# First projection of a diffusion layer: conditioning weights for shift and scale read in eight blocks, norm sums as columns

## The chip, the cores and the metric

The kernel runs as one program on one core of a Trainium2 chip. The core has a matrix engine (TensorE, "PE"), a vector engine (VectorE, "DVE"), a scalar engine with function tables (ScalarE, "ACT"), a general engine (GpSimd, "POOL") and a queue engine (SyncE, "SP"), which here only issues transfers. All work on tiles of up to 128 partitions in on-chip memory (sb); matrix products land in eight banks of 128 x 512 fp32. The metric is the device time of one execution in microseconds (us), the median of several runs.

## The reference

One layer of a diffusion backbone: 256 latent tokens and 256 context tokens of width 1024, all in fp32. What matters here is how the layer's input is made, ahead of three mixing branches and a mixture of experts:

```python
def rmsnorm(x, g):
    y = xf * lax.rsqrt(jnp.mean(xf * xf, axis=-1, keepdims=True) + RMS_EPS)
    return (y * g)
def modulate(h, shift, scale):
    return h * (1 + scale) + shift
# m = silu(c) @ w_ada + b_ada, six vectors of 1024: shift and scale of the mixer come first
# h = modulate(rmsnorm(x, g_mix), shift, scale), for latents with c, for context with c_ctx
zl = split_in(h_lat @ w_in)      # w_in is 1024 x 7936
zc = split_in(h_ctx @ w_in)
```

The first two groups of w_in's columns that the kernel uses are the two forget gates of a gated scan ("ff" and "fb"), 512 columns each.

## The kernel before, in words

The tokens are held transposed: hT has 8 feature blocks (k = 0 to 7, 128 features on the partitions) by 512 tokens. Every weight group is 1024 x 512 (2 MB) and is read into one of three rotating slots of sb. SP issues these reads in the order of the list FRONT; before a slot is taken again it waits until TensorE has used it (`w_used`). TensorE makes a group's output in "fills": a fill is one bank of 128 x 512, the sum over the 8 feature blocks. Each fp32 matmul stands in the trace as two records, a transpose as one. There is no scheduler: each engine's program is written out in order, and semaphores hold the engines together.

The start is this. ACT takes silu of the conditioning vectors (line 511) and squares hT block by block (line 515). TensorE sums the squares over the features with a matrix of ones (line 884), 8 matmuls of 128 x 512, so that each partition holds all 512 sums as a row. ACT takes the root (line 518), DVE the reciprocal of 128 x 512 (line 1142) and multiplies each block by it (line 1166). The conditioning product for shift (w_ada groups ada0, ada1) and scale (ada2, ada3), 512 columns each, is 8 matmuls per group with a stationary operand of only 32 columns (line 695), four such groups of columns of the array running side by side; ACT copies the result (line 535), four transposes bring it onto partitions (line 845), DVE sums the four parts (line 1160), adds the bias and makes the factor A_mix (lines 1171 to 1175), and applies factor and shift to hT in two halves of 256 tokens (line 1179). Half of the features (k = 0 to 3) is served by ada0 and ada2, the other half by ada1 and ada3. So TensorE's order is: ada0, ada2, their transposes, the first half of k for the first three tiles of ff, then ada1, ada3, their transposes, then the second half of k, ff's fourth tile, fb and onwards (lines 889 to 901, matmuls of ff and fb on line 701).

Afterwards TensorE works through the other projections (lines 707 and 711), the scan's levels (line 753; line 774 is a transpose that waits for DVE after group hg), 16 steps of attention, and the branch products; a router with narrow matmuls of 20 columns (line 976) follows, with wide filling matmuls behind it (line 950), and then eight pairs of experts (line 1037), whose weights are 96 reads of 1 MB (line 371). Eight further conditioning groups are summed by POOL from reads of 512 KB behind the later weight groups (line 461).

## Time and profile before

| | |
|---|---|
| runs | 778.0, 776.69, 774.95 us; median 776.69 |
| the profiled execution | 774.23 us, of which its span 772.1 us |
| mean granted clock of TensorE | 0.978 of full speed |
| TensorE busy | 717.2 us, 93% of the span |
| VectorE, ScalarE, GpSimd busy | 287.3, 107.0, 168.6 us |
| chain that ended last | PE 76%, SPq 10%, DMA 7%, DVE 3%, issue 2%, ACT 1% |

The span is the time between the first and the last instruction that the profiler saw. The chain that ended last is the line of work followed back from the end: what stands on it sets the time, what does not is hidden beside it. Busy shares alone say little: TensorE counts as busy 93% of the time, but some of this is at half its clock.

### The profile page before, as it was taken

To read this page: it belongs to the slowest core of one execution; us is meant where nothing else is said; L and a number is where in the kernel's file an instruction comes from. 1 tells how busy PE (TensorE), PEld (TensorE's weight loads), DVE (VectorE), ACT (ScalarE), POOL (GpSimd) and SP (SyncE) were. 2 spreads that over 40 slices of the span, in tenths; PEclk is the share of its full clock that TensorE was granted. 3 is DMA by queue.
4 is the path that set the end of the run, shared out by engine and by line. 5 is a ranking of instruction groups with operands and counts; after the bars stand their busy time and mean duration, and the time that the engine had idled before them with its cause. 6 is when DMAs were issued, how large, how long until landed. Compare 5 with 4: busy or idle time off the path is not lost.

```text
span 772.1 us, 8154 instructions
## 1 busy us (share of the span) xinstructions
PE 717.2 (93%) x3366; PEld 428.6 (56%) x3366; DVE 287.3 (37%) x499; ACT 107.0 (14%) x194; POOL 168.6 (22%) x120
## 2 busy tenths in 40 slices
PE   5889998999999979999999999999999999998873
PEld 2334585666587436767677878746444443443321
DVE  1537434765530083653533332414422211220224
ACT  5010010000000222312111250013000000000013
POOL 0049589747358300060000000000000000000010
PEclk9999998999999989999999999999999999999988
DMA  9875455423055122431232322799799999999991
GB/s 371 372 299 219 156 222 207 178 82 136 1 197 177 25 93 109 151 132 44 109 109 110 109 109 109 318 423 420 282 416 424 423 423 422 421 422 423 422 413 65
DMA packets 25525, 184.21 MB, mean 239 GB/s; under 512 B 2832, under 2 KB 2960, under 8 KB 9360
## 3 DMA queue, kind: packets, MB, share of 16 engines
q1 hardware_dynamic: 23472, 176.56, 57.2%
q10 hardware_dynamic: 1440, 5.01, 1.6%
q0 software_dynamic: 576, 2.10, 0.7%
q8 instruction: 28, 0.46, 0.2%
q14 instruction: 9, 0.07, 0.0%
HBM read 178.95 MB, written 4.72 MB: 238 GB/s over the span
## 4 chain that ended last, share of the span: by engine, by line
PE 76%; SPq 10%; DMA 7%; DVE 3%; issue 2%; ACT 1%; DVEq 0%
PE bank L707 16%; PE bank L1037 11%; PE bank L701 11%; SPq L371 10%; PE bank L711 8%; PE bank L724 5%; DMA sb<-expert_w 4%; PE bank L753 4%; PE bank L730 4%; PE bank L1012 2%; DMA sb<-front_w 2%; PE bank L876 2%; PE bank L855 2%; PE bank L717 2%; PE bank L863 2%
## 5 line engine op out<-in xcount | busy, mean ns | idle before, releaser
L1037 PE MATMUL bank<-sb 128*64 128x512 f32 x768 | 173.2, 608 | 10.1 <-DMA sb<-expert_w 8.9
L707 PE MATMUL bank<-sb 128*128 128x256 f32 x576 | 128.3, 381 | 0.6 <-PE bank L701 0.3
L1037 PEld LDWEIGHTS bank<-sb 128*64 128x64 f32 x768 | 57.0, 140 | 119.5 <-issue 118.5
L707 PEld LDWEIGHTS bank<-sb 128*128 128x128 f32 x576 | 108.1, 190 | 17.9 <-issue 3.8
L501 POOL DMA_INDIRECT sb<-y_rows,slot_rows x4 | 3.9, 984 | 392.3 <-DMA y_rows<-sb 391.4
L701 PE MATMUL bank<-sb 128*128 128x512 f32 x192 | 83.8, 593 | 4.0 <-DVE sb L1179 3.7
L461 POOL TENSOR_TENSOR sb<-sb 128x1024 f32<-128x1024 f32 x32 | 64.6, 2020 | 65.0 <-DMA sb<-ada_w 63.0
L711 PE MATMUL bank<-sb 128*128 128x512 f32 x160 | 70.3, 594 | 0.3 <-PE bank L707 0.3
L1226 DVE COPY sb<-bank 128x512 f32<-128x512 f32 x45 | 29.5, 686 | 106.9 <-PE bank L863 73.6
L701 PEld LDWEIGHTS bank<-sb 128*128 128x128 f32 x192 | 35.9, 190 | 47.8 <-issue 44.5
L711 PEld LDWEIGHTS bank<-sb 128*128 128x128 f32 x160 | 29.8, 190 | 36.0 <-issue 36.0
L1545 DVE TENSOR_TENSOR sb<-sb,bank 128x512 f32<-128x512 f32 x8 | 5.5, 687 | 110.7 <-PE bank L1037 110.7
L724 PE MATMUL bank<-sb 128*128 128x256 f32 x192 | 42.2, 380 | 0.6 <-PE bank L724 0.6
L724 PEld LDWEIGHTS bank<-sb 128*128 128x128 f32 x192 | 36.2, 190 | 6.3 <-issue 1.5
L465 POOL TENSOR_TENSOR sb<-sb 128x512 f32<-128x512 f32 x24 | 35.2, 1468 | 1.9
L466 POOL TENSOR_TENSOR sb<-sb 128x512 f32<-128x512 f32 x24 | 34.8, 1449 | 1.9
L753 PEld LDWEIGHTS bank<-sb 128*128 128x128 f32 x256 | 32.0, 201 | 5.3 <-issue 4.4
L753 PE MATMUL bank<-sb 128*128 128x128 f32 x256 | 33.3, 288 | 0.3 <-PE bank L711 0.3
L1012 PEld LDWEIGHTS bank<-sb 128*128 128x128 f32 x256 | 29.8, 192 | 6.2 <-issue 6.2
L1012 PE MATMUL bank<-sb 128*128 128x128 f32 x256 | 31.7, 278 | 0.0
L1246 DVE COPY_PREDICATED sb<-masks,bank 128x512 f32<-128x512 int8 x28 | 20.5, 734 | 27.6 <-PE bank L753 27.4
L580 ACT ACTIVATE sb<-bank,sb 128x512 f32<-128x512 f32 x32 | 21.8, 685 | 61.0 <-DVE sb L1328 61.0
(228 smaller groups left out, 638.5 us busy)
## 6 DMA issues: line engine op xcount, KB each, us to landing
sb<-expert_w SPq DMA_DIRECT2D x96, 1024.0 KB, 24.8
sb<-front_w SPq DMA_DIRECT2D x24, 2048.0 KB, 8.8
sb<-ada_w SPq DMA_DIRECT2D x32, 512.0 KB, 3.5
y_rows<-sb ACTq DMA_DIRECT2D x7, 512.0 KB, 7.8
sb<-xcT SPq DMA_DIRECT2D x2, 1024.0 KB, 7.4
sb<-na_bias SPq DMA_DIRECT2D x1, 1536.0 KB, 12.0
sb<-front_w SPq DMA_DIRECT2D x1, 1024.0 KB, 8.2
sb<-b_rows SPq DMA_DIRECT2D x1, 1024.0 KB, 11.0
```

The costliest lines, as they stand in the source:

```text
L371: sp.dma_start(slot[s][:, cols], d["expert_w"][row, :, cols]).then_inc((w_in_, w_in_late)[h][s], 16)
L461: link(pool.tensor_tensor(w, w, cvec[:, k0:k0 + PART_K, 0:1].broadcast_to([P, PART_K, 512]), ALU.mult))
L465: link(pool.tensor_tensor(w[:, 0, :], w[:, 0, :], w[:, 1, :], ALU.add))
L466: ins = pool.tensor_tensor(ada_sum[g], ada_sum[g], w[:, 0, :], ALU.add)
L701: ins = pe.matmul(ps[:, :], lhs(w, k, i * P), hT[:, k, :], start=(k == 0), stop=(k == KD - 1))
L707: ins = pe.matmul(ps[:, c * L:(c + 1) * L], lhs(w, k, (2 * i + c) * P), hT[:, k, 0:L], start=(k == 0), stop=(k == KD - 1))
L711: ins = pe.matmul(ps[:, :], hT[:, k, i * P:(i + 1) * P], w[:, k * 512:(k + 1) * 512], start=(k == 0), stop=(k == KD - 1))
L724: ins = pe.matmul(ps[:, c * L:(c + 1) * L], lhs(w, k, (2 * i + c) * P, D), src[:, k, :], start=(k == 0), stop=(k == 3))
L730: ins = pe.matmul(ps[:, :], yT[:, k, i * P:(i + 1) * P], w[:, k * 512:(k + 1) * 512], start=(k == 0), stop=(k == KD - 1))
L753: ins = pe.matmul(ps[:, h * P:(h + 1) * P], kk, qq, start=True, stop=True)
L1012: ins = pe.matmul(banks[i][:, c * P:(c + 1) * P], xn[:, t, (4 * i + c) * P:(4 * i + c + 1) * P], S[:, t, :], start=(t == 0), stop=(t == NT ...
L1037: ins = pe.matmul(bank[e * CAP:(e + 1) * CAP, :], lhsT[:, k, e * CAP:(e + 1) * CAP], slot[pair_[e]][:, o + k * 512:o + (k + 1) * 512], sta ...
```

## The change

Order and shapes change, and every result that the rest of the kernel uses is still made. In the start:

- hT is read in four parts instead of two. ACT squares the even blocks, DVE the odd ones. ACT loads the table of the root ahead of its squares with a one-column instruction.
- The sums of squares are taken with the squares as stationary operand and one column of ones as moving operand: 4 matmuls of one output column per block, 32 in all, into 4 columns of a bank. Root and reciprocal then work on 128 x 4. DVE spreads the result over a diagonal (128 x 512), and one matmul with the matrix of ones makes the row again, which DVE reads from the bank.
- The shift and scale columns of w_ada are laid out as 8 blocks of 1 MB, one per feature block, with 128 columns of shift and 128 of scale. Block c needs 8 matmuls of 256 columns, one ACT copy of 128 x 256, and two matmuls of 2 output columns with a selection matrix `sel`, which transpose and sum at once. DVE then adds the bias to both, makes A_mix and applies them to block c alone.
- The first projection (ff) runs with the feature block as the outer loop and its four tiles inside, into four banks at once. The products of later conditioning blocks stand between its matmuls. ff's weights are read in four parts of 512 KB between the blocks.
- The small constants are read in two parts. The scan's masks are read as int8 in their place, without GpSimd's conversion.
- The four ada groups leave FRONT; the three slots and the ring of expert slots are renumbered.

The diff, cut to its core:

```diff
-FRONT = ["ada0", "ada2", "ff", "ada1", "ada3", "fb", "hq", "hg", "hi", "nk", "nq", "nv", "gq", "gkv"]
+FRONT = ["ff", "fb", "hq", "hg", "hi", "nk", "nq", "nv", "gq", "gkv"]
...
-RING = ((3, 4), (5, 6), (7, 2), (8, 9), (0, 1))
+RING = ((3, 4), (5, 6), (7, 0), (8, 9), (1, 2))
 LAST = PAIRS - 1
 STORED = LAST * P
 
-SLOT_OF = [0, 1, 2, 0, 1] + [n % FSLOTS for n in range(len(FRONT) - 5)]
-USES = [SLOT_OF.count(s) for s in range(FSLOTS)]
-GROUPS = ["ada0", "ada2", "ada1", "ada3", "ff"] + FRONT[5:]
+SLOT_OF = [n % FSLOTS for n in range(len(FRONT))]
+USES = [len([n for n in range(1, len(FRONT)) if SLOT_OF[n] == s]) for s in range(FSLOTS)]
...
-BANK_OF = [5 if f[0] == "ada1" else 6 if f[0] == "ada3" else n % PBANKS for n, f in enumerate(FILLS)]
+FIRST_BANKS = (0, 1, 2, 5, 6)
+BANK_OF = [FIRST_BANKS[n] if n < len(FIRST_BANKS) else n % PBANKS for n in range(len(FILLS))]
...
-        ada_early = at(A0, 2, 512)
+        ada_mix = [at(o, KD, 256) for o in (A0, A0 + 2048, A0 + 4096)]
...
-        masks_wide = at(F0, 2 * (LEVELS - 1), P)
+        ada_mix += [at(F0 + 2048 * i, KD, 256) for i in range(4)]
...
-        rstd_row = at(C0, 512)
+        rstd_diag = at(C0, 4, P)
...
+        ada_rows = at(C0 + 8192, 2, 256)
...
-            for i in range(2):
-                sp.dma_start(hT[:, 4 * i:4 * i + 4, :], d["xcT"][:, 4 * i:4 * i + 4, :]).then_inc(x_in[i], 16)
+            for i in range(4):
+                sp.dma_start(hT[:, 2 * i:2 * i + 2, :], d["xcT"][:, 2 * i:2 * i + 2, :]).then_inc(x_in[i], 16)
+            for k in range(KD):
+                sp.dma_start(ada_mix[k].rearrange("p a b -> p (a b)"), d["ada_mix"][k, :, :]).then_inc(ada_mix_in[k], 16)
+                if k % 2 == 0:
+                    cols = slice(512 * k, 512 * k + 1024)
+                    sp.dma_start(slot[0][:, cols], d["front_w"][0, :, cols]).then_inc(ff_in[k // 2], 16)
+                if k == 4:
+                    sp.dma_start(small[:, SMALL_FIRST:SMALL], d["small_w"][:, SMALL_FIRST:SMALL]).then_inc(small_in, 16)
+            sp.dma_start(masks[:, :, :], d["level_masks"]).then_inc(masks_in, 16)
...
-            pool.wait_ge(masks_in, 16)
-            pool.tensor_copy(masks[:, :, :], masks_wide).then_inc(masks_ready, 1)
...
-            act.dma_start(small, d["small_w"]).then_inc(small_in, 16)
+            act.dma_start(small[:, 0:SMALL_FIRST], d["small_w"][:, 0:SMALL_FIRST]).then_inc(first_in, 16)
             act.wait_ge(c_in, 16)
             act.activation(cvec, cvec, ACT.Silu).then_inc(c_ready, 1)
-            for k in range(KD):
-                if k % 4 == 0:
-                    act.wait_ge(x_in[k // 4], 16)
-                act.activation(sq[:, k, :], hT[:, k, :], ACT.Square).then_inc(sq_ready, 1)
+            act.wait_ge(ones_set, 1)
+            act.activation(warm, ones_now[:, 0:1], ACT.Sqrt)
+            for k in range(0, KD, 2):
+                act.wait_ge(x_in[k // 2], 16)
+                act.activation(sq[:, k, :], hT[:, k, :], ACT.Square).then_inc(sq_by["act"], 1)
             act.wait_ge(rms_ready, 1)
-            act.wait_ge(small_in, 16)
-            act.activation(rstd_row, pv_bank[:, :], ACT.Sqrt, bias=sm("eps"), scale=1.0 / D).then_inc(rms_root, 1)
+            act.wait_ge(first_in, 16)
+            act.activation(rcol, score[1][:, 0:4], ACT.Sqrt, bias=sm("eps"), scale=1.0 / D).then_inc(rms_col, 1)
+            for c in range(KD):
+                act.wait_ge(rows_ready_, c + 1)
+                if c > 1:
+                    act.wait_ge(sel_ready, c - 1)
+                act.activation(ada_rows[:, c % 2, :], shared[c % 2][:, 0:256], ACT.Copy).then_inc(rows_out, 1)
...
+            def ada_block(c):
+
+                pe.wait_ge(ada_mix_in[c], 16)
+                if c > 1:
+                    pe.wait_ge(mod_ready, c - 1)
+                for k in range(KD):
+                    q = 32 * (k % 4)
+                    ins = pe.matmul(shared[c % 2][q:q + 32, 0:256], cvec[:, k, :], ada_mix[c][:, k, :],
+                                    start=(k < 4), stop=(k >= KD - 4))
+                ins.then_inc(rows_ready_, 1)
+
+            def select_streams(c):
+
+                pe.wait_ge(rows_out, c + 1)
+                for j in range(2):
+                    ins = pe.matmul(shared[c % 2][:, 256 + 2 * j:258 + 2 * j], ada_rows[:, c % 2, j * P:(j + 1) * P], sm("sel"),
+                                    start=True, stop=True)
+                ins.then_inc(sel_ready, 1)
+
             pe.wait_ge(ones_set, 1)
             for k in range(KD):
-                pe.wait_ge(sq_ready, k + 1)
-                ins = pe.matmul(pv_bank[:, :], ones_now, sq[:, k, :], start=(k == 0), stop=(k == KD - 1))
+                pe.wait_ge(sq_by["dve" if k % 2 else "act"], k // 2 + 1)
+                for t in range(4):
+                    ins = pe.matmul(score[1][:, t:t + 1], sq[:, k, t * P:(t + 1) * P], ones_now[:, 0:1],
+                                    start=(k == 0 and t == 0), stop=(k == KD - 1 and t == 3))
             ins.then_inc(rms_ready, 1)
             pe.wait_ge(c_ready, 1)
+            pe.wait_ge(first_in, 16)
+            ada_block(0)
+            select_streams(0)
+            pe.wait_ge(diag_ready, 1)
+            pe.matmul(pv_bank[:, :], ones_now, rstd_diag.rearrange("p a b -> p (a b)"), start=True, stop=True)\
+              .then_inc(rstd_ready, 1)
+            ada_block(1)
+            select_streams(1)
+            ada_block(2)
+            for k in range(KD):
+                pe.wait_ge(h_ready, k + 1)
+                if k % 2 == 0:
+                    pe.wait_ge(ff_in[k // 2], 16)
+                for i in range(4):
+                    if i == 2:
+                        if k + 2 < KD:
+                            select_streams(k + 2)
+                        if k + 3 < KD:
+                            ada_block(k + 3)
+                    ins = pe.matmul(banks[BANK_OF[i]][:, :], lhs(slot[0], k, i * P), hT[:, k, :],
+                                    start=(k == 0), stop=(k == KD - 1))
+                    if k == KD - 1:
+                        ins.then_inc(fill_ready, 1)
+            pe.wait_ge(fill_ready, 4)
+            pe.sem_inc(w_used, 1)
             pe.wait_ge(small_in, 16)
-
-            early = range(fill_no("ff"), fill_no("ff") + PBANKS)
-            for first, second in ((0, 2), (1, 3)):
-                fill(fill_no(f"ada{first}"))
-                fill(fill_no(f"ada{second}"))
-                ada_turn(first)
-                ada_turn(second)
-                if first == 0:
-                    for n in early:
-                        fill(n, range(KD // 2))
-            for n in early:
-                fill(n, range(KD // 2, KD))
-            for n in range(early[-1] + 1, fill_no("hg", 1) + 1):
+            for n in range(4, fill_no("hg", 1) + 1):
...
-            dve.wait_ge(small_in, 16)
-
-            lg = sm("lb")
-            dve.tensor_tensor(lb_e, lg, lg, ALU.subtract).then_inc(lb_in, 1)
-            dve.wait_ge(rms_root, 1)
-            link(dve.reciprocal(rstd_row, rstd_row))
+            for k in range(1, KD, 2):
+                dve.wait_ge(x_in[k // 2], 16)
+                dve.tensor_tensor(sq[:, k, :], hT[:, k, :], hT[:, k, :], ALU.mult).then_inc(sq_by["dve"], 1)
+            dve.wait_ge(rms_col, 1)
+            link(dve.reciprocal(rcol, rcol))
+            dve.wait_ge(first_in, 16)
+            dve.tensor_tensor(rstd_diag, ident.unsqueeze(1).broadcast_to([P, 4, P]), rcol.unsqueeze(2).broadcast_to([P, 4, P]),
+                              ALU.mult).then_inc(diag_ready, 1)
...
             b_ada = sm("b_ada")
-            for half in range(2):
-                ks = slice(4 * half, 4 * half + 4)
-                for k in range(4 * half, 4 * half + 4):
-                    dve.tensor_tensor(hT[:, k, :], hT[:, k, :], rstd_row, ALU.mult)
-                add_ada(half)
-                add_ada(2 + half)
-                dve.wait_ge(shared_out, 2 * half + 2)
-                for m in (4 * half, 8 + 4 * half):
-                    ins = dve.tensor_tensor(mod[:, m:m + 4, :], mod[:, m:m + 4, :],
-                                            b_ada[:, m:m + 4].unsqueeze(2).broadcast_to([P, 4, 2]), ALU.add)
-                link(ins)
-                link(dve.tensor_scalar(A_mix[:, ks, :], mod[:, 8 + 4 * half:12 + 4 * half, :], 1.0, None, ALU.add))
-                link(dve.tensor_tensor(A_mix[:, ks, :], A_mix[:, ks, :],
-                                       sm("g_mix")[:, ks].unsqueeze(2).broadcast_to([P, 4, 2]), ALU.mult))
-                for k in range(4 * half, 4 * half + 4):
-                    for s in range(2):
-                        ins = dve.tensor_scalar(hT[:, k, s * L:(s + 1) * L], hT[:, k, s * L:(s + 1) * L],
-                                                A_mix[:, k, s:s + 1], mod[:, k, s:s + 1], ALU.mult, ALU.add)
-                    ins.then_inc(h_ready, 1)
+            dve.wait_ge(rstd_ready, 1)
+            for k in range(KD):
+                dve.tensor_tensor(hT[:, k, :], hT[:, k, :], pv_bank[:, :], ALU.mult).then_inc(v_step, 1)
+                steps[0] += 1
+                dve.wait_ge(sel_ready, k + 1)
+                both = mod[:, k:k + 9:8, :]
+                dve.tensor_tensor(both, shared[k % 2][:, 256:260].rearrange("p (j s) -> p j s", j=2),
+                                  b_ada[:, k:k + 9:8].unsqueeze(2).broadcast_to([P, 2, 2]), ALU.add).then_inc(mod_ready, 1)
+                dve.wait_ge(mod_ready, k + 1)
+                link(dve.scalar_tensor_tensor(out=A_mix[:, k, :], in0=mod[:, 8 + k, :], scalar=1.0,
+                                              in1=sm("g_mix")[:, k:k + 1].broadcast_to([P, 2]), op0=ALU.add, op1=ALU.mult))
+                for s in range(2):
+                    ins = dve.tensor_scalar(hT[:, k, s * L:(s + 1) * L], hT[:, k, s * L:(s + 1) * L],
+                                            A_mix[:, k, s:s + 1], mod[:, k, s:s + 1], ALU.mult, ALU.add)
+                ins.then_inc(h_ready, 1)
+            dve.wait_ge(small_in, 16)
+            lg = sm("lb")
+            dve.tensor_tensor(lb_e, lg, lg, ALU.subtract).then_inc(lb_in, 1)
...
+    wa = a["w_ada"][0][:, 0:2 * D].reshape(KD, P, 2, KD, P)
+    ada_blocks = wa.transpose(3, 1, 0, 2, 4).reshape(KD, P, KD * 256)
```

On TensorE the head of the program reads as follows before; 884 are the sums of squares, 695 the conditioning products, 845 their transposes, 701 the first projections and 707 the next ones.

```order
L884 MATMUL bank<-sb 128x512 x8
L695 MATMUL bank<-sb 32x512 x16
L845 MATMUL bank<-sb 128x128 x8
L701 MATMUL bank<-sb 128x512 x12
L695 MATMUL bank<-sb 32x512 x16
L845 MATMUL bank<-sb 128x128 x8
L701 MATMUL bank<-sb 128x512 x52
L707 MATMUL bank<-sb 128x256 x64
```

Now 901 are the sums of squares, 885 a conditioning block, 893 its selection, 909 the row of norms and 924 the first projection.

```order
L901 MATMUL bank<-sb 128x1 x32
L885 MATMUL bank<-sb 32x256 x8
L893 MATMUL bank<-sb 128x2 x2
L909 MATMUL bank<-sb 128x512
L885 MATMUL bank<-sb 32x256 x8
L893 MATMUL bank<-sb 128x2 x2
L885 MATMUL bank<-sb 32x256 x8
L924 MATMUL bank<-sb 128x512 x2
L893 MATMUL bank<-sb 128x2 x2
L885 MATMUL bank<-sb 32x256 x8
L924 MATMUL bank<-sb 128x512 x4
L893 MATMUL bank<-sb 128x2 x2
```

Eight wide matmuls became 32 of one column, and three of the eight conditioning blocks stand ahead of the first projection; the other five stand inside it.

On DVE the head before has the wide reciprocal (1142) and serves four blocks at a time.

```order
L1142 RECIPROCAL sb<-sb 128x512
L1166 TENSOR_TENSOR sb<-sb 128x512 x4
L1160 TENSOR_REDUCE sb<-bank 128x8 x2
L1171 TENSOR_TENSOR sb<-sb 128x8 x2
L1174 TENSOR_SCALAR sb<-sb 128x8
L1175 TENSOR_TENSOR sb<-sb 128x8
L1179 TENSOR_SCALAR sb<-sb 128x256 x8
```

Now it starts with its half of the squares (1170) and the diagonal (1174), and lines 1194 to 1204 stand once for each of the eight blocks.

```order
L1170 TENSOR_TENSOR sb<-sb 128x512 x4
L1172 RECIPROCAL sb<-sb 128x4
L1174 TENSOR_TENSOR sb<-sb 128x512
L1194 TENSOR_TENSOR sb<-sb,bank 128x512
L1198 TENSOR_TENSOR sb<-bank,sb 128x2x2
L1201 SCALAR_TENSOR_TENSOR sb<-sb 128x2
L1204 TENSOR_SCALAR sb<-sb 128x256 x2
```

A block of hT is finished by four kinds of instruction in a row instead of after the fourth block of its half.

## Rows read from the trace of the kernel before

**Rows 1.** Chain of waits in order of time: start us, length us, what ran.

```profile
2.12 18.07 DMA sb<-front_w
20.24 1.97 PE bank L695 x16
22.35 1.21 PE bank L845 x8
...
25.38 10.54 PE bank L701 x24
35.92 1.90 PE bank L695 x16
...
43.13 17.45 PE bank L701 x40
60.86 27.72 PE bank L701 x64
...
121.79 1.97 PE bank L774 x8
...
644.62 5.57 SPq L371
```

**Rows 2.** Timeline, 6 to 18 us: start us, length us, engine, line.

```profile
6.47 0.42 ACT L511 ACTIVATE sb<-sb 128x256 f32<-128x256 f32 x1 [3.52 <-DMA sb<-cvec]
6.79 2.17 ACT L515 ACTIVATE sb<-sb 128x512 f32<-128x512 f32 x4
...
7.55 8.97 PE L884 MATMUL bank<-sb 128*128 128x512 f32 x16 [7.55 <-ACT sb L515]
...
17.28 3.35 DVE L1142 RECIPROCAL sb<-sb 128x512 f32<-128x512 f32 x1 [6.49 <-ACT sb L518]
```

**Rows 3.** The timeline of TensorE's weight loads (PEld) under line 884.

```profile
10.24 0.34 PEld L884 LDWEIGHTS bank<-sb 128*128 128x128 f32 x1 [0.52 <-issue]
...
12.07 0.19 PEld L884 LDWEIGHTS bank<-sb 128*128 128x128 f32 x1 [0.24 <-issue]
```

**Rows 4.** Stretches: width; PE, PEld, DVE, ACT, POOL busy; clock; DMA; GB/s.

```profile
531.00:532.00 1.00, 1.00 (x12) 1.00 (x11) 0.48 (x1) 0.77 (x3) 0.00 (x0) 1.00 0.98 410
533.00:534.00 1.00, 1.00 (x9) 1.00 (x9) 0.00 (x0) 0.47 (x1) 0.00 (x0) 0.77 1.00 418
534.00:535.00 1.00, 1.00 (x4) 0.75 (x4) 0.46 (x3) 0.17 (x1) 0.00 (x0) 0.50 0.99 410
537.00:538.00 1.00, 1.00 (x4) 0.52 (x3) 0.86 (x7) 0.04 (x1) 0.00 (x0) 1.00 0.98 406
```

**Rows 5.** The same view, the first wide matmuls of line 884.

```profile
7.50:11.40 3.90, 3.85 (x5) 1.81 (x6) 0.17 (x1) 2.44 (x5) 0.00 (x0) 1.00 1.05 445
11.40:16.40 5.00, 5.00 (x12) 1.90 (x10) 0.00 (x0) 2.50 (x4) 0.00 (x0) 1.00 1.03 439
```

**Rows 6.** The same view, after PE's idle time before 121.79.

```profile
123.70:125.70 2.00, 1.98 (x10) 1.95 (x10) 0.69 (x1) 0.00 (x0) 1.84 (x3) 0.50 0.59 219
125.70:127.70 2.00, 2.00 (x13) 2.00 (x13) 0.84 (x2) 0.00 (x0) 1.92 (x2) 0.58 0.02 4
```

**Rows 7.** Groups by line and shape, 0 to 61 us: busy, mean ns.

```profile
L1179 DVE TENSOR_SCALAR sb<-sb 128x256 f32<-128x256 f32 x16 | 5.3, 408 | 0.1
L1166 DVE TENSOR_TENSOR sb<-sb 128x512 f32<-128x512 f32 x8 | 5.0, 685 | 0.0
...
L535 ACT ACTIVATE sb<-bank 128x512 f32<-128x512 f32 x4 | 2.4, 592 | 19.5 <-PE bank L695 19.5
...
L511 ACT ACT_TABLE_LOAD x1 | 1.3, 1283 | 1.7 <-PEq L1790 1.7
...
L1183 DVE RECIPROCAL sb<-sb 128x8 f32<-128x8 f32 x1 | 0.2, 199 | 0.0
```

**Rows 8.** The DMA issues by line: count, KB each, median us to landing.

```profile
sb<-xcT SPq DMA_DIRECT2D x2, 1024.0 KB, 7.4
...
sb<-small_w ACTq DMA_DIRECT2D x1, 672.5 KB, 9.4
```

More of the change, by code:

```diff
@@ L117 @@
 LEVELS = 8
-SHARED = [("ada", g) for g in (0, 2, 1, 3)] + [("kc", i) for i in range(4)]
+SHARED = [("kc", i) for i in range(4)]
 SHARED += [(f"lev{v}", i) for v in range(LEVELS) for i in range(4)] + [("s0", i) for i in range(2)]
@@ L237, in build @@
         lb_e, lb_p = keep(8), keep(8)
+        rcol, warm = keep(4), keep(1)
         g_ms = keep(24)
@@ L273, in sem @@
             return ctx.enter_context(nc.semaphore(name))
-        x_in = [sem("x_in0"), sem("x_in1")]
+        x_in = [sem(f"x_in{i}") for i in range(4)]
+        ada_mix_in, ff_in = [sem(f"ada_mix_in{i}") for i in range(KD)], [sem(f"ff_in{i}") for i in range(4)]
+        first_in = sem("first_small_in")
+        rows_ready_, rows_out, sel_ready, mod_ready = [sem(n) for n in ("ada_rows_ready", "ada_rows_out", "sel_ready", "mod_ready")]
+        sq_by = {"act": sem("sq_by_act"), "dve": sem("sq_by_dve")}
+        rms_col, diag_ready, rstd_ready = sem("rms_col"), sem("diag_ready"), sem("rstd_ready")
         c_in, small_in, bias_in, masks_in, xnat_in, glast_in = [sem(n) for n in (
@@ L674, in take_slot, with fill @@
             def take_slot(n):
-                pe.wait_ge(w_in_[SLOT_OF[n]], 16 * (len(earlier(n)) + 1))
+                pe.wait_ge(w_in_[SLOT_OF[n]], 16 * len([m for m in earlier(n) + [n] if m]))
             def lhs(w, k, c, width=512):
                 return w[:, k * width + c:k * width + c + P]
-            def fill(n, ks=range(KD)):
+            def fill(n):
                 name, i, _ = FILLS[n]
@@ L685, in fill @@
                 before = [m for m in range(n) if BANK_OF[m] == BANK_OF[n]]
-                if before and ks[0] == 0:
+                if before:
                     wait_emptied(pe, before[-1])
@@ L689, in fill @@
                 w = slot[SLOT_OF[g]]
-                if i == 0 and ks[0] == 0:
+                if i == 0:
                     take_slot(g)
-                if name[:3] == "ada":
+                if name in ("fb", "nk"):
                     for k in range(KD):
-                        q = 32 * (k % 4)
-                        ins = pe.matmul(ps[q:q + 32, :], cvec[:, k, :], w[:, k * 512:(k + 1) * 512],
-                                        start=(k < 4), stop=(k >= KD - 4))
-                elif name in ("ff", "fb", "nk"):
-                    for k in ks:
-                        if name == "ff" and i == 0:
-                            pe.wait_ge(h_ready, k + 1)
                         ins = pe.matmul(ps[:, :], lhs(w, k, i * P), hT[:, k, :], start=(k == 0), stop=(k == KD - 1))
-                    if ks[-1] < KD - 1:
-                        return
                 elif name in ("hq", "hg", "nq") or name[:4] == "gate":
@@ L1154, in add_ada @@
                 else:
[L1155 to L1159 removed]
+                    parts, dst = ps[:, :].rearrange("p (c q) -> p c q", c=4), mod[:, 4 * g:4 * g + 4, 0]
                     dve.tensor_reduce(dst, parts, AX.X, ALU.add).then_inc(shared_out, 1)
@@ L1644 @@
 SMALL = 0
-for _name, *_dims in (("ident", P), ("ones", P), ("upto", P), ("iota", CAP), ("eps", 1), ("limits", MAXPASS - 1),
-                      ("rank", NE), ("first_slot", NE), ("b_ada", 48), ("g_mix", KD), ("g_ffn", KD), ("lb", 8), ("hg_g", 1),
+for _name, *_dims in (("ident", P), ("sel", 2), ("eps", 1), ("b_ada", 48), ("g_mix", KD),
+                      ("ones", P), ("upto", P), ("iota", CAP), ("limits", MAXPASS - 1),
+                      ("rank", NE), ("first_slot", NE), ("g_ffn", KD), ("lb", 8), ("hg_g", 1),
                       ("gqn", HD), ("gqn_swapped", HD), ("gkn", HD), ("gkn_swapped", HD),
@@ L1650 @@
     SMALL += int(np.prod(_dims))
+SMALL_FIRST = SM["ones"][0]
 def columns(v):
@@ L1670, in shape_constants @@
     return {
-        "ident": np.eye(P, dtype=f), "ones": np.ones((P, P), f),
+        "ident": np.eye(P, dtype=f), "sel": (i[:, None] % 32 == np.arange(2)[None, :]).astype(f), "ones": np.ones((P, P), f),
         "upto": (i[:, None] <= i[None, :]).astype(f),
@@ L1682, in level_masks @@
     i = np.arange(P)
-    out = np.zeros((P, 2 * (LEVELS - 1), P), np.float32)
+    out = np.zeros((P, 2 * (LEVELS - 1), P), np.int8)
     for v in range(LEVELS - 1):
@@ L1740 @@
     for name in FRONT:
-        if name[:3] == "ada":
-            s = ada[int(name[3:])]
-        elif name[:4] == "gate":
+        if name[:4] == "gate":
             s = gate[int(name[4:])]
```

51 lines of the change are left out of this document (17 added, 34 removed).

## Prediction

> **What bounds the kernel now.** I read the chain of waits first. From 20.24 to 644.62 it runs nearly all on TensorE, with short waits for DVE and ACT; only at 644.62 do reads of expert weights take over [rows 1]. The change touches what lies before the group fb, whose first matmul starts at 60.86. From there on both programs have the same matmuls in the same order, the slots keep their distance to one another, and the expert reads are started by TensorE's progress. So the question is one number: when does fb start? A shift there passes through to the end almost unchanged.
>
> The first stretch has these pieces [rows 1]: conditioning weights for two groups land at 20.2, their products take 1.97, transposes and DVE follow, and the first projection starts at 25.38. It runs 10.54 us, stops for the other conditioning groups (35.92 to 43.13, 7.2 us), runs 17.45 us and ends at 60.58. From 25.38 to that end are 35.2 us, then 0.3 to fb. Beside it the sums of squares occupy TensorE from 7.55 to 16.52, and the wide reciprocal holds DVE from 17.28 for 3.35 us [rows 2]; both end before the weights are there and 25.38 is set by the weights alone.
>
> **What the first projection holds.** Its 24 and 40 records take 10.54 and 17.45 us, 28.0 together, 0.44 each at the full clock [rows 1]; this work stays. Inside it now stand five conditioning blocks and six selections. A block is half of a group's columns, so half of 1.97: 1.0 us. A selection is four records; narrow records pass at 12 per us at the full clock [rows 4], so 0.4 us. That is 5.0 + 2.4 = 7.4 us against 7.2 before, and the whole is 35.4 against 35.2. The new loop order changes no record. DVE's work for a block is one multiply of 0.69, two small ones near 0.2 and two of 0.41 [rows 7], 1.9 us beside 4.4 us of TensorE per block: hidden. If that cover went, TensorE would wait for DVE at each block, which needs DVE at over twice these durations.
>
> The reads: tokens 2 MB, conditioning 8 MB, ff 2 MB and the constants, whose one read was 672.5 KB [rows 8], are 13.4 MB up to block 7. At 439 GB/s [rows 5] that is 31 us; with the start of the queues block 7 is there at about 35. It is used in the middle of k = 4, which is 19 us after the projection starts, so near 48 by the sum below. SP issues these reads with no wait between them, and fb and hq queue right behind them, at about 41 and 46: fb is wanted at 60 or later. SP then passes to the 512 KB parts and, where it waits for POOL, only hg's read and what follows it are behind; hg is wanted over 40 us later. The cover is 13 us or more everywhere, and I cost the reads at nothing.
>
> **What stands ahead of the first projection.** This is where the sum is made.
>
> 1. Start of the sums. Silu ends at 6.89 [rows 2]. Then ACT loads the root's table, 1.28 [rows 7], runs its one-column instruction (0.2, the size of small instructions) and squares block 0: four squares take 2.17, so 0.55 each [rows 2]. Block 0 is ready at 8.9 (7.5 before). The later blocks come every 0.55 us from two engines and are not waited for.
> 2. 32 narrow matmuls, 64 records. Each needs its own load of 128 columns, and one column of output does nothing to cover it. The nearest rows are the router's matmuls of 20 columns: 12 in a us at the full clock [rows 4], so 0.09 each. But what is the clock? The first five records of the old sums took 0.78 on average where twelve later ones took 0.42, and the loads 0.34 against 0.19 [rows 5, 3]: TensorE starts at its lower level, 1.2 GHz, although the clock column says 1.00 there, and rises after 4 us of wide matmuls. After idle time in the middle of the kernel the same is seen in the column: 0.50 after the start at 121.79, full again only at about 127.4 [rows 1, 6]. And in the router the opposite: TensorE is busy all the time with narrow records, and between 533 and 534 its granted clock falls to 0.50; it is back at 1.00 by 537, after wide matmuls were put behind them [rows 4]. I read that narrow records don't hold the clock up, and so will not raise it. At the low level 64 x 0.18 = 11.5 us. From both sides: 64 x 0.09 = 5.8, and 64 x 0.246 = 15.7 by the slow transposes at 121.79 (1.97 for eight). I take 11.5, whose shape is nearest. The sums end at 20.4, against 16.5 before.
> 3. From there the norms: root and reciprocal on four columns 0.25 and 0.20, diagonal 0.69 [rows 7], 1.2 us in all. Beside them TensorE does block 0 (2.0 at the low clock), ACT copies it (0.4, between the 0.59 of twice the columns [rows 7] and a small one), and the selection of four records with its latency takes half of the 1.21 of eight transposes [rows 1], 0.6, low clock 1.2. Only then comes the matmul for the row, two wide records, 1.7. Together 5.3: the row of norms is there at 25.7. In place of the 3.35 reciprocal a chain through three engines has come, in TensorE's order behind block 0.
> 4. Then block 1, its copy and selection, and block 2: 3.0 us at the full clock, 5.6 at the low. The wide row matmul and the blocks should raise the clock about here; I take the middle, 4.3. DVE has block 0 of hT ready 1.9 us after the row, earlier than that. The first projection starts at 30.0.
> 5. 30.0 + 35.4 + 0.3 = 65.7 for fb, against 60.86: 4.9 us later.
>
> The early mask conversion by POOL goes, 672 KB less are read, ACT evacuates four tiles of ff together instead of one after the other: all of it lies beside fb's 27.7 us [rows 1] and costs or gives nothing; without that cover the four copies would cost 4 x 0.6.
>
> The Trainium skill ("TensorE: Matmul & The Clock Gate", section on LDWEIGHTS) gives a load's time by its columns alone over 1.2 GHz, an estimate of 107 ns for 128 columns whatever the clock. By it the 64 records would take 6.8 us. The trace disagrees with it: the loads took 0.34 and 0.19 at the two levels [rows 3]. What follows if loads don't slow here is the second rival.
>
> The same page (section on the clock gate) says that the throttled state is the default and that activity releases it; this case's trace agrees, with 0.78 and 0.42 per record [rows 5].
>
> The profiled execution took 774.2 us (span 772.1 and 2.1 around it); with 4.9 it would be 779.1. The median before is 776.69, 2.5 above that profile, so for a median I forecast 781.6.
>
> **The rivals.**
> - *The clock rises in the sums (not slower).* If the narrow records count as work, TensorE is at 2.4 GHz 4 us after 8.9, as it was after 7.55. Then 22 records take 4.0, the other 42 take 3.8: end at 16.7. What follows runs at the full clock, 2.9 to the row and 3.0 to the projection, at 22.6; fb starts at 58.3, 2.6 us earlier: 774.1. It decides between the two signs if the clock is up by about the 50th of the 64 records. For it: the loads keep TensorE busy. Against it: so they did in the router, where the clock fell [rows 4].
> - *Narrow records are no slower at the low clock.* 5.8 us in spite of it, end at 14.7; with steps 3 and 4 unchanged fb starts at 60.0, 0.8 earlier: 775.9. Against it: rows 3.
> - *Narrow records are fast and the clock is up as well.* 14.7 + 5.9 = 20.6 for the projection, fb at 56.3, 4.6 earlier: 772.1. It needs the low start of rows 5 not to come again.
> - *The low clock reaches into the first projection.* Steps 3 and 4 are broken by waits for ACT and DVE. If they don't raise the clock, the projection starts at 31.3 and its first 4 us do half the work: 2.0 more, fb at 69.0, 8.1 later: 784.8. For it: at 121.79 the rise took 5.6 us of unbroken work [rows 1, 6].
> - *A read is late.* Smaller pieces might move slower than 439 GB/s, but block 7 would have to come 13 us late to matter. Small.
>
> **How the numbers follow.** The forecast case has 0.45, with its own range of 779.5 to 783.5. The rise in the sums 0.15, no slowing 0.12, both fast 0.08, the low clock into the projection 0.15, and 0.05 for the rest, half to each side. The range 773 to 787 leaves out little but the fast end and a low clock with the slower bound of step 2. A shift of under 0.5%, 3.9 us, can't be told from no change here. About two thirds of the forecast case lie above it, with the low-clock rival and a little more: 0.49 slower. Faster needs the both-fast case and a piece of the first rival: 0.12. The rest, 0.39, is the same.
>
> **What would show it.** In the changed profile the 64 records of the sums should be some 0.18 apart and end near 20.4; a spacing of 0.09 from the fifth us on is the first rival. The reciprocal is no longer seen. The row matmul should end near 25.7, and the first wide projection record start near 30 at a granted clock of 1.00 (0.50 there is the low-clock rival). From it to fb should be 35.7 us, without waits for DMA. If fb starts earlier than 60.86, the forecast is wrong in step 2 or 3; if fb moves and the end does not move with it, the claim that the rest follows is wrong.

## The result, and the profile after

The changed kernel takes 783.29 us (median of 4 runs, 780.95 to 784.9) against 776.09 for the kernel before (4 runs): a ratio of 1.0088, 95% interval 1.0054 to 1.0122. It is slower by 7 us; 4.9 were forecast. The profiled execution took 784.9 us (span 783.1).

The chain of waits of the changed kernel, in order of time (start us, length us, what ran). 901 are the sums of squares, 885 a conditioning block, 893 a selection, 909 the row of norms, 924 the first projection, 703 fb:

```profile
8.31 13.79 PE bank L901 x64
22.10 1.91 PE bank L885 x16
...
24.46 1.01 PE bank L893 x4
25.48 1.92 PE bank L909 x2
27.39 1.91 PE bank L885 x16
...
29.76 1.02 PE bank L893 x4
30.78 1.86 PE bank L885 x16
32.64 3.71 PE bank L924 x4
36.35 0.65 PE bank L893 x4
37.00 1.00 PE bank L885 x16
38.00 3.63 PE bank L924 x8
...
61.85 8.70 PE bank L924 x20
...
70.84 27.72 PE bank L703 x64
```

fb starts at 70.84 where it started at 60.86 [rows 1]. The sums take 13.79 us and end at 22.10. Everything up to 36.35 has the lengths of the lower clock: a block 1.91, where the one at 37.00 takes 1.00; four wide records 3.71, where eight take 3.63 at 38.00. TensorE gets to 2.4 GHz only behind the first four wide records of the projection.

The counterpart of [rows 5] in the changed kernel (width; busy us and instructions of PE, PEld, DVE, ACT, POOL; clock; DMA; GB/s):

```profile
7.50:11.40 3.90, 3.09 (x15) 3.12 (x15) 1.69 (x3) 2.34 (x5) 0.00 (x0) 1.00 1.03 426
11.40:16.40 5.00, 5.00 (x25) 5.00 (x25) 0.00 (x0) 0.00 (x0) 0.00 (x0) 1.00 1.03 424
```

25 instructions stand in the five us where 12 wide ones stood. The clock column says 1.00 throughout, here up to 36.35 and in the kernel before in its first stretch, 7.50 to 11.40, while the records have the lengths of the lower clock. At the start the column can't be read, the lengths of the records can.

Further on nothing new happens. The same pieces in the rest of the chain: nv's last fills, and the point where reads of expert weights take over:

```profile
256.33 20.62 PE bank L711 x48
...
651.90 2.75 SPq L384
```

The first stood at 247.42 before, so 8.9 of the 10.0 us are still there; the second at 644.62 [rows 1], 7.3 earlier; at the end of the span it is 11.0. So the later parts add or take up to some 4 us of their own. Span minus fb's start is 711.2 before and 712.3 now. Over all the profiles below it lies between 709.1 and 714.5 and follows no edit: the start decides, but a shift of 2 or 3 us between single profiles does not have to come from it.

### The profile page after: what moved, and what is told of

The parts are those of the page before. It is cut to its first block, busy times and chain, and to the rows that moved or that the text cites. A ratio compares the mean times of both kernels' runs of the same rounds, so it can differ in the third digit from the quotient of the medians.

```text
span 783.1 us, 8439 instructions
## 1 busy us (share of the span) xinstructions
PE 727.4 (93%) x3496; PEld 443.7 (57%) x3496; DVE 288.6 (37%) x508; ACT 105.5 (13%) x195; POOL 166.0 (21%) x119
## 4 chain that ended last, share of the span: by engine, by line
PE 78%; SPq 10%; DMA 5%; DVE 3%; issue 2%; ACT 1%; DVEq 0%
PE bank L707 16%; PE bank L1068 11%; SPq L384 10%; PE bank L711 8%; PE bank L703 7%; PE bank L724 5%; DMA sb<-expert_w 4%; PE bank L753 4%; PE bank L924 4%; PE bank L730 4%; PE bank L1043 2%; PE bank L873 2%; PE bank L852 2%; PE bank L717 2%; PE bank L901 2%; PE bank L860 2%
## 5 line engine op out<-in xcount | busy, mean ns | idle before, releaser
L1068 PE MATMUL bank<-sb 128*64 128x512 f32 x768 | 168.3, 594 | 15.0 <-DMA sb<-expert_w 13.6
L1068 PEld LDWEIGHTS bank<-sb 128*64 128x64 f32 x768 | 55.3, 137 | 121.3 <-issue 120.2
L707 PEld LDWEIGHTS bank<-sb 128*128 128x128 f32 x576 | 108.1, 190 | 17.9 <-issue 3.8
L711 PE MATMUL bank<-sb 128*128 128x512 f32 x160 | 70.3, 594 | 0.4 <-PE bank L707 0.4
L703 PE MATMUL bank<-sb 128*128 128x512 f32 x128 | 55.8, 593 | 0.3 <-PE bank L924 0.3
L711 PEld LDWEIGHTS bank<-sb 128*128 128x128 f32 x160 | 29.8, 190 | 36.1 <-issue 36.1
L703 PEld LDWEIGHTS bank<-sb 128*128 128x128 f32 x128 | 23.9, 190 | 29.3 <-issue 29.3
L724 PEld LDWEIGHTS bank<-sb 128*128 128x128 f32 x192 | 36.2, 190 | 6.3 <-issue 1.5
L753 PEld LDWEIGHTS bank<-sb 128*128 128x128 f32 x256 | 31.7, 199 | 5.4 <-issue 4.5
L1043 PEld LDWEIGHTS bank<-sb 128*128 128x128 f32 x256 | 29.8, 192 | 6.2 <-issue 6.2
L924 PE MATMUL bank<-sb 128*128 128x512 f32 x64 | 31.1, 633 | 0.0
## 6 DMA issues: line engine op xcount, KB each, us to landing
sb<-na_bias SPq DMA_DIRECT2D x1, 1536.0 KB, 11.5
```

The source lines that it names most:

```text
L703: ins = pe.matmul(ps[:, :], lhs(w, k, i * P), hT[:, k, :], start=(k == 0), stop=(k == KD - 1))
L707: ins = pe.matmul(ps[:, c * L:(c + 1) * L], lhs(w, k, (2 * i + c) * P), hT[:, k, 0:L], start=(k == 0), stop=(k == KD - 1))
L711: ins = pe.matmul(ps[:, :], hT[:, k, i * P:(i + 1) * P], w[:, k * 512:(k + 1) * 512], start=(k == 0), stop=(k == KD - 1))
L724: ins = pe.matmul(ps[:, c * L:(c + 1) * L], lhs(w, k, (2 * i + c) * P, D), src[:, k, :], start=(k == 0), stop=(k == 3))
L753: ins = pe.matmul(ps[:, h * P:(h + 1) * P], kk, qq, start=True, stop=True)
L924: ins = pe.matmul(banks[BANK_OF[i]][:, :], lhs(slot[0], k, i * P), hT[:, k, :], start=(k == 0), stop=(k == KD - 1))
```

## The experiments

Where an edit builds on another, its diff is against that one, and each diff is cut to its core. The other parts of the change (squares on two engines, the early table load, the masks as int8, the renumbered slots) are in all the edits of the changed kernel and were not undone one by one. "fb" is the start of fb's first matmul in the profile. Ratios are against the kernel before on the same chip, with 95% intervals.

### Wide sums in the changed kernel

```diff
-                for t in range(4):
-                    ins = pe.matmul(score[1][:, t:t + 1], sq[:, k, t * P:(t + 1) * P], ones_now[:, 0:1], ...)
+                ins = pe.matmul(pv_bank[:, :], ones_now, sq[:, k, :], start=(k == 0), stop=(k == KD - 1))
...
-            link(dve.reciprocal(rcol, rcol))
-            dve.tensor_tensor(rstd_diag, ident..., rcol..., ALU.mult)
+            link(dve.reciprocal(rstd_row, rstd_row))
```

> The changed kernel with one part undone: the sums of squares are again 8 wide matmuls (ones stationary, squares moving, 512 columns), the root and reciprocal again work on 128 x 512, the diagonal and its matmul go. The blocks, the loop order and the reads stay. Theory (narrow records run at the low clock and leave it low for all that follows): the sums start at 8.3 and end near 17.3 (five records of 0.85, eleven of 0.43), root 0.7, reciprocal 3.35 and DVE's 1.9 for block 0 bring the first projection to 23.3 at the full clock, and fb starts near 59, 12 us before the changed kernel's 70.8 and 2 before the old 60.9. Median near 772 to 774. Rival (64 loads cost 0.215 us each whatever the clock, and the block scheme itself keeps the clock low): only the 4.8 us of the sums come back, the blocks' records stay at the low speed up to 4 us into the projection, fb starts near 66.

Measured: 773.41 us, ratio 0.9953 (0.9934 to 0.9971). One part undone, and the change turns from slower to faster than before. Its chain of waits (900 are the wide sums, 919 the projection):

```profile
8.38 10.02 PE bank L900 x16
...
18.43 0.69 ACT sb L529
...
19.15 3.37 DVE sb L1167
...
23.45 1.07 PE bank L885 x16
24.52 3.60 PE bank L919 x4
28.12 0.34 PE bank L893 x4
...
62.40 27.72 PE bank L703 x64
```

The sums end at 18.40, the projection starts at 24.5, 8.1 us before the changed kernel's. Theory and rival both missed in part: fb is at 62.40, not 59 or 66. Blocks run at the full clock (1.07 at 23.45), but TensorE is idle in part beside the reciprocal, and the four records at 24.52 are slow again; the granted clock is 0.50 from about 24.5 to 27.

This profile does not show the gain itself: it is of the slowest of the 11 executions (775.58), and its fb is 1.5 us later than in the kernel before. The gain stands in the times of all executions.

### Filling matmuls ahead of the narrow sums

```diff
+            for _ in range(8):
+                pe.matmul(score[0][:, 0:384], ones_now, at(C0 + 512, 384), start=True, stop=True)
             for k in range(KD):
```

> The changed kernel with 8 wide filling matmuls (384 columns of constants) on TensorE from 1.4 us on, ahead of the narrow sums; nothing else differs. Theory (the clock sets the narrow records' spacing, and narrow records let it fall): the sums start near 8.4 at about 0.11 us per record, after about 4 us the spacing doubles to 0.215, they end near 18 in place of 22.1, and all behind them runs as before the edit: fb near 67, 4 us earlier. Rival 1 (a load costs 0.215 whatever the clock): the spacing is 0.215 from the first record, fb at 70.8. Rival 2 (narrow records only fail to raise the clock but do hold it): the sums end near 15.3, all that follows is at the full clock, fb near 58.

Measured: 779.34 us, ratio 1.0032 (1.0009 to 1.0055), fb at 64.19. Stretches of 1 us within the narrow sums, which start at 8.67 (columns as above):

```profile
9.40:10.40 1.00, 1.00 (x11) 1.00 (x10) 0.69 (x1) 0.63 (x1) 0.00 (x0) 1.00 1.00 426
10.40:11.40 1.00, 1.00 (x11) 1.00 (x10) 0.00 (x0) 0.00 (x0) 0.00 (x0) 1.00 0.95 393
11.40:12.40 1.00, 1.00 (x9) 1.00 (x9) 0.00 (x0) 0.00 (x0) 0.00 (x0) 0.82 1.05 426
12.40:13.40 1.00, 1.00 (x6) 1.00 (x6) 0.00 (x0) 0.00 (x0) 0.00 (x0) 0.50 1.07 418
```

The granted clock is 1.00 at first and falls to 0.50 near 12.0. Since 8.67 TensorE has run nothing but narrow records, and PE and PEld are busy all the time. The 64 records take 10.27 us in place of 13.79. If the low spacing is 0.2155 (13.79 / 64), 32 of them fit behind 12.0 and the other 32 passed at 0.105: the clock halves them. Rivals 1 and 2 both fall. fb is 3 us earlier than the 67 of the theory, because here the clock is up again by the second selection: it takes 0.61 at 26.48, the projection's first four records 1.91.

### The narrow sums alone, in the kernel before

```diff
-                ins = pe.matmul(pv_bank[:, :], ones_now, sq[:, k, :], ...)
+                for t in range(4):
+                    ins = pe.matmul(score[1][:, t:t + 1], sq[:, k, t * P:(t + 1) * P], ones_now[:, 0:1], ...)
```

> The kernel before with one part of the change alone: the sums as 32 narrow matmuls, root and reciprocal on four columns, the diagonal and its matmul (placed behind group ada0). Everything else as before. Theory: the sums end near 21.4 in place of 16.5, ada0, the row and ada2 follow at the low clock (3.9, 1.9, 3.9 us), the first projection starts near 34.7 and its first 4 us are slow: fb near 72, 11 us after the old 60.9; median near 787. Rival (the blocks and the outer loop over k are what costs): the late end of the sums is mostly hidden behind the weights that land at 20.2, fb near 63 to 64.

Measured: 781.27 us, ratio 1.0049 (1.0032 to 1.0066). Its chain (887 the sums, 697 a conditioning group, 703 the first projection and fb):

```profile
7.79 13.78 PE bank L887 x64
21.57 3.61 PE bank L697 x16
...
31.55 12.23 PE bank L703 x24
...
68.62 27.72 PE bank L703 x64
```

By the ratios this one part costs more than half of the loss (0.49% of 0.73% to 0.88%); in the profile fb is 7.8 us later. I had forecast 11, and a median of 787: the clock rose during the row (1.17 at 25.32), so group ada2 took 1.90. It did not stay up. TensorE was idle for 1.84 us ahead of the projection, its granted clock is 0.50 from 33 to 35, and the 24 records take 12.23 where they took 10.54 [rows 1].

### Wide sums and filling matmuls ahead

```diff
+            for _ in range(8):
+                pe.matmul(score[0][:, 0:384], ones_now, at(C0 + 512, 384), start=True, stop=True)
```

> The changed kernel with wide sums (as in the first of these runs) and the 8 wide filling matmuls ahead of them. Theory: the sums run at the full clock from 8.3, end near 15.2, the first projection starts near 21.2 and fb near 57, 2 us before the first of these runs and 4 before the kernel before; median near 771. Rival (something else than the clock, the conditioning reads or DVE, holds the first projection): fb where the first of these runs has it.

Measured: 772.48 us, ratio 0.9934 (0.9907 to 0.996), fb at 61.23. The 57 of the theory is missed by 4. The sums take 6.88 and end at 16.23, but block 2 takes 1.93 and the first four records of the projection 3.71: TensorE's granted clock falls near 20.2, at the end of DVE's reciprocal (16.97 to 20.34), and most of what was won ahead is lost behind.

### The changed kernel twice more

> The changed kernel once more, unaltered, for its time against the kernel before on the same chip as the next three, and for a second look at its first 70 us. Theory (narrow sums at the low clock every time): the 64 records again take 13.8 us, fb starts between 69 and 71, ratio near 1.009. Rival (the first profile was a slow draw of something that varies): sums shorter by 2 us or more, fb below 68, ratio under 1.006.

> The changed kernel, unaltered, a third look at its first 70 us. Theory (the 64 narrow records always run at the low clock, but the point at which the clock rises behind them varies between executions): 13.8 us for the records again, fb between 67 and 71, and the execution's time follows fb: some 781 for 67.7, some 785 for 70.8. Rival (the spread of the executions comes from later parts): the time does not follow fb.

Measured: 781.33 us, ratio 1.0073 (1.0044 to 1.0102); and one execution of 782.72. The chain of the second profile:

```profile
8.50 13.78 PE bank L901 x64
...
29.95 0.61 PE bank L893 x4
...
31.55 1.92 PE bank L924 x4
...
67.66 8.39 PE bank L703 x19
```

The records take 13.78 (third profile 13.79), so they run at the low clock each time. But the selection at 29.95 and block 2 behind it are fast: the clock rose near 29.9, not 36.4, and fb is at 67.66 (third: 67.38). The three executions took 784.9, 781.3 and 782.7 us for fb at 70.84, 67.66 and 67.38: the order of the last two is not that of fb, by 1.4 us, so the later parts vary as well. Of the second run's expectation the records came true and fb (69 to 71) did not; of the third run's, theory and rival are each half right.

### Holding the clock through narrow sums

```diff
+                elif k % 2:
+                    pe.matmul(score[0][:, :], ones_now, sq[:, 0, :], start=True, stop=True)
```

> The changed kernel with 6 wide filling matmuls ahead of the narrow sums and one wide filling matmul (two records, 0.86 us) after every 16 narrow records, three in all. Theory (narrow records follow the clock, and wide work keeps it up): 64 x 0.105 + 3 x 0.86 = 9.3 us of sums, end near 17.6, chain behind them at the full clock (6.0), the first projection near 23.6, fb near 59.5: 11 us before the changed kernel although 2.6 us of work were added. Median near 773. Rival (the fall can't be held off by so little, or the chain behind the sums is slow for another reason): sums end at 19 or later, or the first projection starts more than 8 us behind them; fb at 64 or later.

Measured: 782.39 us, ratio 1.0058 (1.0037 to 1.008), fb at 68.15. The rival is right. Its chain (903 sixteen narrow records, 908 a filling matmul):

```profile
8.10 1.95 PE bank L903 x16
10.04 0.97 PE bank L908 x2
11.01 1.68 PE bank L903 x16
12.69 1.86 PE bank L908 x2
14.55 3.21 PE bank L903 x16
17.76 1.92 PE bank L908 x2
19.68 3.20 PE bank L903 x16
```

The first 32 narrow records pass at 0.105 to 0.12, the next 32 at 0.20: the clock falls in spite of a wide matmul after every sixteen, and the filling work is paid in full.

### Wide sums, the clock held to the projection

```diff
-            for _ in range(8):
+            for _ in range(6):
...
             ada_block(0)
+            pe.matmul(score[0][:, :], ones_now, sq[:, 0, :], start=True, stop=True)
             select_streams(0)
```

(and the same behind block 1)

> The changed kernel with wide sums, 6 wide filling matmuls ahead of them, and one filling matmul each in the two waits for ACT between the sums and the first projection. Theory (what was left in the run with wide sums and filling matmuls was the clock falling while DVE takes the wide reciprocal): sums end near 15.2, the first projection starts near 21.3 and runs at 0.43 per record from its first one, fb near 57, 4 us before that run; median near 769. Rival (the first records of the projection are slow because of DVE or bank changes, not the clock): its first four records again take 3.6 us or more, fb near 60.

> The run with wide sums and held clock once more, unaltered, on the same chip as the run with added squares, so that the two can be compared. Expected: fb again near 57.6, ratio near 0.993.

Measured: 771.31 us, ratio 0.9928 (0.9904 to 0.9953), and again 770.73, ratio 0.9915 (0.9895 to 0.9935). The chain of the first:

```profile
8.20 7.15 PE bank L902 x16
...
15.37 0.70 ACT sb L529
...
16.09 3.36 DVE sb L1171
...
20.39 1.07 PE bank L885 x16
21.46 1.91 PE bank L923 x4
...
57.57 18.69 PE bank L703 x43
```

The projection starts at 21.46, its first four records take 1.91, half of the changed kernel's 3.71, and fb is at 57.57 (57.52 the second time) where 57 was expected; the time was expected at 769. The slow first records were the clock. This version beats both kernels.

### Control: filling matmuls in the kernel before

```diff
+                if first == 0:
+                    for _ in range(2):
+                        pe.matmul(score[0][:, :], ones_now, sq[:, 0, :], start=True, stop=True)
```

(behind ada0 and ahead of the first projection, and six at the start)

> Control: the kernel before with the same 6 filling matmuls at the start, two after ada0 and two ahead of the first projection, in its idle time; nothing of the change. Theory (its start is bound by the weights that land at 20.2, and the profile showed the full clock in the gaps): fb stays near 60.9, ratio 0.997 to 1.000. Rival (the filling matmuls alone give the gain, and the blocks nothing): ratio near that of the run with wide sums and held clock.

Measured: 774.17 us, ratio 0.9968 (0.995 to 0.9986), fb at 60.85. In the profile fb starts within 0.01 us of where it was, yet the time is 0.3% better. The profiled execution (772.05) is 2.2 us shorter than that of the kernel before (774.23), and this stands far behind the filled gaps, at DVE's multiply of 128 x 1024 behind group hg. Here, and then in the kernel before:

```profile
118.46 1.22 DVE sb L1230
```

```profile
118.44 2.69 DVE sb L1223
```

GpSimd's sum next to it begins at 118.48 here, just after DVE, and at 118.16 in the kernel before, just ahead of it. The last fills of nv then start at 245.27, not at 247.42. So these two profiles trace no gain to the filling. Whether other executions of the kernel before lose the clock in the gaps that are filled here, no profile shows, and where the 0.3% comes from stays open. In the kernel before, filling is worth 0.3% (0.1% to 0.5%); in the changed kernel with wide sums it moved fb from 62.40 to 57.57.

### Squares added first

```diff
+                if k > 1:
+                    link(dve.tensor_tensor(sq[:, 1, :], sq[:, 1, :], sq[:, k, :], ALU.add))
...
+            for t in range(4):
+                ins = pe.matmul(score[1][:, t:t + 1], sq[:, 1, t * P:(t + 1) * P], ones_now[:, 0:1], ...)
```

> The changed kernel with the columns kept but the eight blocks of squares first added up on DVE (seven adds of 128 x 512), so that TensorE needs 4 narrow matmuls in place of 32; 12 filling matmuls at the start, one behind block 0, the narrow matmuls behind block 0's selection. Theory (what hurts in the columns is the number of narrow records at a low clock, not the chain root, reciprocal, diagonal, row): DVE's adds end near 14.1, the 8 records near 15, the row near 17.1, the first projection starts near 19.2 and fb near 55.4, 2 us before the run with wide sums and held clock; ratio near 0.990. Rival (a clock that falls in the waits for DVE, or DVE's links take more than counted): the projection starts at 21 or later or its first four records take over 2.5 us, fb no earlier than 57.5.

Measured: 770.71 us, ratio 0.9928 (0.9904 to 0.9952), fb at 56.37 where 55.4 was expected. On the same chip the version with wide sums has 0.9915 (0.9895 to 0.9935): the two can't be told apart, though fb is 1.15 us earlier. The timeline of its PE (908 the narrow sums, 927 the projection):

```profile
14.45 1.05 PE L908 MATMUL bank<-sb 128*128 128x1 f32 x8
...
20.20 1.98 PE L927 MATMUL bank<-sb 128*128 128x512 f32 x4
```

Eight narrow records take 1.05, so the column form itself is sound when it has few records. TensorE waits 0.6 us here for the read of block 1, until 16.1.

### The loop order undone

```diff
-                for i in range(4):
-                    ins = pe.matmul(banks[BANK_OF[i]][:, :], lhs(slot[0], k, i * P), hT[:, k, :], ...)
+                ins = pe.matmul(banks[BANK_OF[0]][:, :], lhs(slot[0], k, 0), hT[:, k, :], ...)
+            for i in range(1, 4):
+                for k in range(KD):
+                    ins = pe.matmul(banks[BANK_OF[i]][:, :], lhs(slot[0], k, i * P), hT[:, k, :], ...)
```

(against the version with wide sums and held clock)

> The run with wide sums and held clock, with the loop order of the first projection undone: tile 0 over all eight blocks first (the selections and blocks between its matmuls), then tiles 1 to 3. Theory (the outer loop over blocks hides the reads of the later blocks): tile 0 has to wait for block 7, which lands at about 35; it ends near 39, three tiles of 6.9 us follow, fb starts near 60.2, 2.6 later. Rival (the order is worth nothing because everything is there in time): fb at 57.6. If the waits let the clock fall, up to 2 us more.

Measured: 777.36 us, ratio 1.0006 (0.9986 to 1.0025). Its chain (921 tile 0, 926 tiles 1 to 3):

```profile
7.82 22.92 DMA sb<-ada_mix
...
30.79 1.94 PE bank L885 x16
32.72 1.65 PE bank L921 x2
...
42.20 20.61 PE bank L926 x48
...
63.11 16.98 PE bank L703 x39
```

The order over blocks outside is worth 5.5 us of fb's start (63.11 against 57.57), and as much as the whole gain over the kernel before. I had priced 2.6. The selections and blocks stand here in TensorE's program ahead of tile 0's matmul for each k (the diff leaves them out); with this loop order no run has another placement. TensorE is idle for 3.3 us until block 5 is there at 30.79 and loses the clock (1.94 for the block, 1.65 for two records), and tile 0 ends at 42.20, not 39.

## Why the prediction was right, point by point

- *The question is when fb starts, and the rest follows.* Right. fb moved by 6.5 to 10.0 us in three profiles, the ratios give 5.7 and 6.8 us (0.73% and 0.88%), and the time from fb to the end kept within 3.5 us of 711 under all edits.
- *Step 1, start of the sums at 8.9.* It was 8.31: the conditioning vector landed 0.8 us earlier. The read behind it on its queue is shorter now; whether that is the cause, no run tests.
- *Step 2, the clock.* The mechanism is shown. Narrow records run at half speed at the low clock (0.2155 against 0.105) and let a full clock fall. The size was off: 64 x 0.18 = 11.5 was forecast, 13.79 measured. I had read 0.09 from the instruction count of a stretch of 1 us [rows 4]; the count holds the instructions cut by both edges too (eight records of the same router start 0.81 us before the next ones, 530.04 to 530.85, so 0.10 each). Of the excess of the first profile over the forecast, 10.0 against 4.9, this term is 2.3, step 1 gives back 0.6, step 4 adds 0.95 and the projection 2.5. In the second profile, where fb is 2.0 later than the 65.7 forecast, it is this term almost alone: 2.3, less 0.4 from step 1 and 0.3 from step 4, plus 0.4 from the projection.
- *Step 3, 5.3 us from the sums to the row.* Measured 5.29 (22.10 to 27.39), 5.30 in the second profile.
- *Step 4, 4.3 us to the projection.* Measured 5.25, 3.97 and 3.97: the clock decides here, as said. The 4.3 was the middle of two cases and no reading; that it lies near two of three profiles is luck.
- *The first projection, 35.4 us.* 37.9 in the first profile, of which 1.9 are its slow first four records, 35.8 in the second. Per block it is 0.34 + 1.00 + 3.63 = 4.97. So the rival of the low clock that reaches into the projection, given 0.15, is what the first profile shows; the other two are the forecast case.
- *Reads and DVE cost nothing.* No read and no DVE step stands in the chain between 8.31 and 70.84. DVE's cover was thin, though: its work on one of the last blocks takes 4.7 us beside GpSimd's sums (its pairs on line 1204 start at 58.67 and 63.33), not 1.9, against 4.97 of TensorE per block. Its last pair ends at 66.12, and at 0.435 us per record the last block's first matmul starts near 67.1 (an estimate): 1 us to spare. The reads had more cover than I gave them, block 7 being used at 56.88 and not near 48. That this cover hangs on the loop order the last experiment shows.
- *The rivals.* The clock does not rise in the sums, even helped; narrow records are slower at the low clock, by 2.05.

What the forecast did not see is that the rest of the change was worth 0.5% (0.7% to 0.9% with filling matmuls, which alone give the kernel before 0.3%), hidden under the loss from the sums: with wide sums the change is faster than the kernel before. I had summed the projection's stretch as equal (35.4 against 35.2) and the start as the place of all the change, but not asked what each part would do without the other.

## What to carry to other kernels

A matmul with a wide stationary operand and one column of output costs its weight load, and many of them let TensorE's clock fall and keep it low for the wide work behind them; here a 3.4 us reciprocal was saved, and the first projection started at 31.3 to 32.6 where it started at 24.5 with wide sums. Count records before trading columns for them, add up first what can be added elsewhere, and look at the length of the records at the start of a kernel rather than at its clock column. When a change has several parts, price each alone: one may carry the gain and another lose it.

## What the runs showed of the hardware

- With a wide matmul after every sixteen narrow records, the granted clock was 1.00 when the sums began at 8.1, fell to 0.50 near 12.6 and stayed there to about 29.7, although PE was idle for no more than 0.5 us at a time.
- DVE instructions on 128 x 256 took longer beside GpSimd. Two in the changed kernel's timeline, before GpSimd's sums and beside them (columns: start, length of both, engine, line):

```profile
37.43 0.73 DVE L1204 TENSOR_SCALAR sb<-sb 128x256 f32<-128x256 f32 x2
```

```profile
58.67 2.79 DVE L1204 TENSOR_SCALAR sb<-sb 128x256 f32<-128x256 f32 x2
```

The same pair takes 0.73 us and 2.79 us, GpSimd being busy 4.76 of the 5 us from 58 to 63. The multiply of 128 x 512 that reads a bank (line 1194) is not slower there: 0.68 at 38.08, 0.67 at 61.37. No run takes GpSimd's work away. With TensorE's 4.97 us per block it still stays hidden; a projection of two tiles per block has 0.34 + 1.00 + 1.81 = 3.15 us per block and, by this estimate, would not hide DVE's 4.7.
- In the profiles of the control and of the kernel before, the engine that began second took longer: DVE's multiply takes 2.69 us where GpSimd's sum began 0.28 us ahead of it, and 1.22 where GpSimd's began 0.02 us behind; GpSimd's sum then takes 2.96 in place of 1.90.
